# Slot lists ahead of the sort, two whole units in front, and gates after the copies in a two-layer hybrid transformer block with a mixture of experts

## The reference

```python
N_EXPERTS = 64; TOP_K = 6; D_EXPERT = 384; ROUTED_SCALE = 2.5
def swiglu(x, w_gu, w_down):
    g, u = jnp.split(x @ w_gu, 2, axis=-1)
    return (jax.nn.silu(g) * u) @ w_down
# moe_ffn(h, router_w, router_bias, w_gu, w_down, shared_gu, shared_down):
# "Sigmoid top-k routing with selection bias, normalised gates, SwiGLU experts, plus a shared expert."
```

## Time and profile before

| | us |
|---|---|
| median of 3 runs | 2852.13 (2843.32 to 2856.85) |
| time of the profiled execution | 2859.29 |
| span of its trace | 2857.5 |
| TensorE busy in it | 2446.7 |
| VectorE busy in it | 739.8 |
| ScalarE busy in it | 443.8 |
| GpSimd busy in it | 323.4 |

### The profile page before, as it was taken

The page is one execution under the profiler, slowest core; times in us unless marked ns, Lnnn a source line. Parts: engine busy times, 40 slices in busy tenths (PEclk is TensorE's granted clock), DMA queues, the critical chain, the costliest instruction groups (busy, mean ns, idle before and its releaser), DMA issues. The chain is left out here.

```text
span 2857.5 us, 36782 instructions
## 1 busy us (share of the span) xinstructions
PE 2446.7 (86%) x15205; PEld 1334.6 (47%) x15205; DVE 739.8 (26%) x1589; ACT 443.8 (16%) x901; POOL 323.4 (11%) x380
## 2 busy tenths in 40 slices
PE   4999978898989998988985798999897888888885
PEld 2457834554544444444432355875543434443332
DVE  1373523336111111111110445454410111111111
ACT  1233232310000000000000132343000000000000
POOL 0006200000011111110100002400011110010000
PEclk8999987898999999999997899999899999999998
DMA  8000077434699999999995600013599999999993
GB/s 296 30 15 32 3 274 244 164 121 154 246 426 423 412 398 416 400 402 396 394 409 214 222 30 30 4 64 112 226 415 427 421 421 421 415 410 413 411 415 135
DMA packets 126587, 775.99 MB, mean 272 GB/s; under 512 B 36760, under 2 KB 45096, under 8 KB 69968
## 3 DMA queue, kind: packets, MB, share of 16 engines
q1 hardware_dynamic: 103376, 735.75, 63.9%
q0 software_dynamic: 23040, 37.82, 3.5%
HBM read 770.98 MB, written 44.44 MB: 285 GB/s over the span
## 5 line engine op out<-in xcount | busy, mean ns | idle before, releaser
L1419 PE MATMUL banks<-arena,htreg 128*64 128x384 f32 (+1 forms) x4288 | 928.3, 524 | 182.8 <-DMA arena<-in_exp_w_gu 169.6
L1419 PEld LDWEIGHTS banks<-arena,htreg 128*64 128x64 f32 (+1 forms) x4288 | 455.9, 157 | 624.4 <-issue 403.9
L1440 PE MATMUL banks<-arena,modreg 128*64 128x512 f32 (+1 forms) x1608 | 436.2, 602 | 20.7 <-issue 16.7
L2150 DVE TENSOR_TENSOR modreg<-modreg,banks 128x384 f32<-128x384 f32 x80 | 44.3, 554 | 1058.3 <-ACT modreg L1712 1058.2
L1440 PEld LDWEIGHTS banks<-arena,modreg 128*64 128x64 f32 (+1 forms) x1608 | 153.4, 149 | 246.2 <-issue 241.6
L2439 POOL DMA_INDIRECT htreg<-h_d,lsg x74 | 76.3, 1031 | 1064.3 <-PE banks L1400 920.4
L989 PE MATMUL banks<-arena,htreg 128*128 128x512 f32 (+3 forms) x480 | 159.7, 492 | 0.0
L2285 DVE COPY modreg<-banks 128x512 f32<-128x512 f32 x74 | 51.2, 692 | 317.6 <-PE banks L1440 317.6
L1712 ACT ACTIVATE modreg<-banks 128x384 f32<-128x384 f32 x80 | 39.2, 491 | 602.3 <-PE banks L1419 602.3
L2445 POOL DMA_INDIRECT y_d<-modreg,lst x74 | 73.4, 992 | 475.1 <-DVE modreg L2285 474.5
L989 PEld LDWEIGHTS banks<-arena,htreg 128*128 128x128 f32 x480 | 90.0, 191 | 65.5 <-issue 61.5
(11 more groups left out here) (393 smaller groups left out, 2228.3 us busy)
## 6 DMA issues: line engine op xcount, KB each, us to landing
arena<-in_exp_w_gu SPq DMA_DIRECT2D x256, 1536.0 KB, 23.6
arena<-in_exp_w_down SPq DMA_DIRECT2D x128, 1536.0 KB, 23.6
modreg<-in_w_mod SPq DMA_DIRECT2D x40, 1024.0 KB, 5.0
arena<-y_d SPq DMA_DIRECT2D x6, 3072.0 KB, 12.7
modreg<-mod_d SPq DMA_DIRECT2D x20, 512.0 KB, 6.2
arena<-in_w_in SPq DMA_DIRECT2D x4, 2048.0 KB, 9.2
arena<-in_w_out SPq DMA_DIRECT2D x2, 4096.0 KB, 14.7
arena<-in_w_mod SPq DMA_DIRECT2D x6, 1024.0 KB, 9.3
```

The lines of the kernel that those rows point to most:

```text
L1419: last = mm(gu_bank(n, half)[rows, 0:DE], src[:, k, rows], up4[q][:, i, DE * half:DE * (half + 1)], start=(k == 0), stop=(k == KD - 1))
L1440: last = mm(ps[4 + half][rows, :], actT[:, k, rows], dn3[q][:, k, 512 * half:512 * half + 512], start=(k == 0), stop=(k == KE - 1))
```

## The change

It reorders work at the start of each layer's experts; no arithmetic is added or removed.

- `work(l)` puts two whole units in front in both layers. Layer 0 has that already; layer 1 becomes `S S w w p p p p p p p p p p p p p p w ...`. The first two routed units then need ranks 0 and 1 only, which the sort's first round gives.
- VectorE does the sort's first round right after the counts, signals it, makes the slot lists, and does rounds 2 to 8 after them. SyncE waits for the second signal before the loads of r2.
- In layer 1 TensorE makes the slot lists between S0's down projection and S1's projections, and r0's transposes come between S1's projections and S1's `act_transposed` and down projection.
- On VectorE r0's transposes are copied before the gates are made; in layer 1 also before S1's output is copied.

```diff
@@ work(l)
         EARLY = 2
+        FIRST = 2
...
-            order = [whole.pop(0) for _ in range(NOUT[l] - EARLY)]
+            order = [whole.pop(0) for _ in range(FIRST)]
@@ SyncE, the loop over CHUNKS
                     if n not in experts:
+                        if n == ROUTED_AT[l][FIRST]:
+                            sp.wait_ge(sorted_ready.sem, sorted_ready.at(l, 2))
@@ TensorE
-                unit_up(0, between=positions if n_t == 2 else None)
-                if n_t > 2:
+                if n_t == 2:
+                    unit_up(0, between=positions)
+                    ranks()
+                    act_transposed(0)
+                    unit_down(0)
+                    lists_by_expert()
+                    lists_by_unit()
+                    unit_up(1)
+                    unit_transposed(EARLY)
+                    act_transposed(1)
+                    unit_down(1)
+                else:
+                    unit_up(0)
                     positions()
-                act_transposed(0)
-                unit_down(0)
-                ranks()
-                unit_up(1, between=lists_by_expert if n_t == 2 else None)
-                if n_t > 2:
+                    act_transposed(0)
+                    unit_down(0)
+                    ranks()
+                    unit_up(1)
                     lists_by_expert()
-                lists_by_unit()
-                act_transposed(1)
-                unit_down(1)
-                unit_transposed(EARLY)
+                    lists_by_unit()
+                    act_transposed(1)
+                    unit_down(1)
+                    unit_transposed(EARLY)
@@ VectorE
+                def sorted_round(j):
+                    link(dve.max(out=next8, in_=left_of[0]))
+                    ins = dve.max_index(out=eid[:, 8 * j:8 * j + 8], in_max=next8, in_values=left_of[0])
+                    if j in (0, NE // 8 - 1):
+                        ins.then_inc(sorted_ready.sem, 1)
+                        dve.wait_ge(sorted_ready.sem, sorted_ready.at(l, 1 if j == 0 else 2))
...
+                sorted_round(0)
...
-                src = key
-                for j in range(NE // 8):
...
-                    if j == 3 and n_t == 2:
-                        unit_times(0)
-                shared_out(0)
+                if n_t == 2:
+                    unit_times(0)
+                else:
+                    shared_out(0)
                 dve.wait_ge(rank_psum.sem, rank_psum.at(l, 1))
...
                 ts(lsg1[:, 0:U_], lst1[:, 0:U_], 3, None, ALU.logical_shift_right).then_inc(lists_ready.sem, 1)
-                unit_times(1)
-                shared_out(1)
-
-                for i in range(n_t):
-                    link(tt(ohp, onehot[:, i], bc(scores[:, i, :], 1, TOPK), ALU.mult))
...
+                if n_t == 2:
+                    shared_out(0)
+                else:
+                    unit_times(1)
+                for j in range(1, NE // 8):
+                    sorted_round(j)
+                if n_t == 2:
+                    unit_times(1)
+
+                def gates_made():
+                    for i in range(n_t):
...
-                unit_copied(EARLY)
+                if n_t == 2:
+                    unit_copied(EARLY)
+                    shared_out(1)
+                else:
+                    shared_out(1)
+                    unit_copied(EARLY)
+                gates_made()
                 overflow_addresses()
```

More of the change, by code:

```diff
@@ L617, in build @@
         chunk_loaded = [sig(f"chunk_loaded{q}", [len(in_slot(l, q)) for l in LAYERS], 16) for q in range(SLOTS)]
-        sorted_ready = sig("sorted_ready", one)
+        sorted_ready = sig("sorted_ready", [2] * DEPTH)
         lo_used = sig("lo_used", NW)
@@ L2183, in _ @@
                 ts(beats[lo64], key[lo64], keycol[lo64], None, ALU.is_lt).then_inc(beats_ready.sem, 1)
+                left_of = [key]
+                def sorted_round(j):
[5 more added lines that the diff above has]
+                    else:
+                        link(ins)
+                    if j < NE // 8 - 1:
+                        link(dve.match_replace(out=left, in_to_replace=next8, in_values=left_of[0], imm_value=-1e9))
+                        left_of[0] = left
+                sorted_round(0)
                 link(ts(row64[lo64], key[lo64], keycol[lo64], None, ALU.is_gt))
@@ L2226, in _ @@
                 ts(lsg1[:, 0:U_], lst1[:, 0:U_], 3, None, ALU.logical_shift_right).then_inc(lists_ready.sem, 1)
-                unit_times(1)
-                shared_out(1)
-                for i in range(n_t):
-                    link(tt(ohp, onehot[:, i], bc(scores[:, i, :], 1, TOPK), ALU.mult))
-                    link(red(gate[:, i, 0:TOPK], ohp, AX, ALU.add))
-                link(red(gatesum[:, nt_], gate[:, nt_, 0:TOPK], AX, ALU.add))
-                link(dve.reciprocal(gatesum[:, nt_], gatesum[:, nt_]))
-                link(stt(gate[:, nt_, 0:TOPK], gate[:, nt_, 0:TOPK], ROUTED, bc(gatesum[:, nt_], 2, TOPK),
-                         ALU.mult, ALU.mult))
+                if n_t == 2:
[8 more added lines that the diff above has]
+                    for i in range(n_t):
+                        link(tt(ohp, onehot[:, i], bc(scores[:, i, :], 1, TOPK), ALU.mult))
+                        link(red(gate[:, i, 0:TOPK], ohp, AX, ALU.add))
+                    link(red(gatesum[:, nt_], gate[:, nt_, 0:TOPK], AX, ALU.add))
+                    link(dve.reciprocal(gatesum[:, nt_], gatesum[:, nt_]))
+                    link(stt(gate[:, nt_, 0:TOPK], gate[:, nt_, 0:TOPK], ROUTED, bc(gatesum[:, nt_], 2, TOPK),
+                             ALU.mult, ALU.mult))
                 def overflow_addresses():
```

## The result

The changed kernel took 2860.98 us in the median (2854.53 to 2869.22) where the one before took 2852.13; the ratio is 1.0033, 95% interval 1.0021 to 1.0046. A second measurement gave 1.0018 (1.0004 to 1.0031). So it is slower by 5 to 9 us, less than the 0.5% that I called a difference, and on the side that was forecast (+5.3 us, 2857.4).

The account below looks back on a forecast made before the run. The stream of expert weights over DMA was taken to bound layer 1; layer 0's -4.6 us and layer 1's +9.9 us sum to +5.3 us on the median of 2852.1, giving 2857.4 us, range 2845 to 2868.

Parts of the forecast that it names:

- The bound and the ring behind U: Layer 1: weights set the pace; eight buffer slots free too slowly behind two whole units, so the stream runs 9.9 us later.
- U: Layer 1: start of the first routed unit's projections on TensorE, forecast at 2061.2 instead of 2059.03.
- c14: Layer 1: the fourteenth load of expert weights, which opens the full rate; forecast to flow from U + 37.4, 2098.6.
- The first load: Layer 1: the first expert load goes at about 2018.1 instead of 2026.35, 8.2 us earlier.
- The gather: Layer 1: the first routed unit's gather lands behind the weight loads at 2050.2, bounds 2046.4 and 2052.9.
- c6 and c7: Layer 1: sixth and seventh loads of expert weights, forecast to drain by 2049.9, with the gather landing behind them.
- Layer 0: Start of layer 0's experts: 4.2 us from VectorE's new order plus 0.4 from earlier slot lists, 4.6 us gained.
- The step that had VectorE free at 708.4: Layer 0: after copies, gates and overflow addresses VectorE is free at 708.4, so shared S2 starts at 710.3, not 714.54.
- The early start: Rival, layer 1: the ring never runs dry and 8.2 us of earlier weights stand; total -12.8 us, 2839; chance 0.07.
- The slow clock: Rival, layer 1: TensorE stays at 1.2 GHz through the first two routed units; total +17 us, 2869; chance 0.12.
- The gather did not come early: Rival, layer 1: gather lands early, U near 2058, layer 1 +6.8, sum +2 us, 2854; chance 0.22.
- its gain gone: Rival, layer 0: VectorE's longer queue takes all of the gain; total +9.9 us, 2862; chance 0.06.

Follow-up runs that it names:

- Kernel 2: The kernel before with one edit: two whole units lead in layer 1; ratio 1.0034.
- kernels 1: The changed kernel, but in layer 1 the first routed unit's transposes stand behind S1's down projection again and S1's output is copied first; ratio 1.0006 to before.
- kernel 6: The changed kernel, but in layer 1 SyncE holds the sixth and seventh loads until the first two routed units' gathers have landed; ratio 0.9998 to before.
- kernel 4: The changed kernel, but in layer 1 all eight sort rounds stand ahead of the slot lists and SyncE waits for the last; ratio 1.0050 to before.
- kernel 5: The kernel before with gates behind the copies and overflow addresses behind the first routed unit's product, in both layers; ratio 0.9978.
- kernel 7: The changed kernel's layer 0 with layer 1 of the kernel before (the sort's first round placed ahead of five small operations); ratio 0.9985 to before.
- 8: Kernel 7 with gates behind the copies in layer 1 too and the overflow addresses late in both layers; ratio 0.9963 to before, 2840.92 us.
- kernels 3: The kernel before with one edit: the first routed unit's transposes are copied before the gates are made, in both layers; ratio 0.9981.
- 9: Kernel 8 with, in layer 1, the sixth load held until the first routed unit's gather has landed; ratio 0.9951 to before, 2837.95 us.

## Why the prediction was right, point by point

**The bound and the ring behind U: right.** I said that c14 would flow from U + 37.4, that is at 2098.6 on the clock of the kernel before, 9.9 us late after a credit. The whole units' share of that is the difference in the table's last column but one, 6.4 us (748.6 against 742.3 on average) where my rows gave 7.7. Kernel 2 shows it alone. The early loads are worth nothing beyond what they do to U: 0.6 us at most for 8.1 us, by kernels 1 and 2.

**The first load:** 8.2 us earlier was forecast, 8.7 measured.

**The gather: right, by the rows rather than by the page of the Trainium skill.** I took 2050.2, on the clock of before, for its landing; it landed at 2051.4 (2036.8 + 14.6, the shift between the two traces at S0). With c6 and c7 held it takes 4.4 us from its issue (kernel 6). With two loads issued just ahead it takes 8.3, and 6.4 in kernel 4, where the first of the two had gone 5.9 us before it and not 2.7. Behind the full backlog it takes 9.5 to 9.7 (kernels 5, 7 and 8, where TensorE waited for it and so shows the landing). So the loads in flight set it. The round robin between rings of the Trainium skill ("DMA: Bandwidth & Descriptors", Queues, rings and completion order), as I read it, would have had it land near 2047: no trace here agrees. Even with no weights in flight it took 4.4 us. So my lower bound of 2.7 us was too low, too. It was of a gather that moved no rows: in the 20 us around one of the two, from 640 to 660 us of the kernel before, the queue of the gathers moved 0.00 MB.

**U: right in sum.** 2061.2 forecast, 2061.7 found, with errors of about 1 us each way in the terms, which is luck. I had r0's transposes at 1.16 us and S1's down projection at 8.46; they took 1.97 and 7.25. What I wrote of the 8.46, that it follows from the small gaps before it, was too simple: the same instructions took 8.46 us in kernels 3 and 9 and 5.39 in kernels 5, 7 and 8. Where they are fast TensorE waits for the gather instead, and r0's projections are slow behind that wait (12.84 to 13.08 us in kernels 5, 7 and 8; 10.54 in kernels 3 and 9). That hid in the kernel before, where both ended together, 47.5 us after S0's start.

**Layer 0: right in size, for partly wrong reasons.** I forecast -4.6 us. The trace keeps 3.4 us by r1, kernel 7 measured 4.3 (0 to 8.6 by its interval), and the average of the layer's length over the six kernels with just this layer 0 is 917.6 against 921.1 of the two with the old one, though single traces differ by 6 us. So a gain of some 4 us is likely and not shown clear of the noise. The step that had VectorE free at 708.4, "a little after TensorE has done r0's projections", was off: it fits r0 at the slow clock, 12.49 us. With the gap ahead of it down to 1.38 us r0 ran at 10.59, TensorE was done sooner and then stood for 4.03 us for VectorE, and S2's first half ran slow for it, 8.30 us. S2 still started 6.3 us sooner, where I had 4.6, and lost 2.9 of it to the slow half. The gates and overflow addresses in VectorE's queue cost that; with the addresses moved away, in kernel 5, the half took 5.43 us.

**The sum:** -3.4 and +8.7 give +5.3 by the marks, the forecast's +5.3, but that match is luck: the forecast was -4.6 and +9.9, and the two misses of 1.2 us cancel. It also takes layer 0 at r1's start; at the end of that layer the same two traces differ by only 0.5 us (920.33 and 919.81), which would give +8.2. The two ratios say +9.4 and +5.1. What of the first is more than the marks show is not explained.

**Rivals.** The early start did not carry. The slow clock did not last through r0 and r1: it was 1.00 from 2046 to 2082. The gather did not come early. In none of the traces with the changed layer 0 is its gain gone at r1's start.

## What to carry to other kernels

Where transfers bind a stage and a ring of buffers feeds it, an earlier first transfer is worth only what the ring can hold; past that the time hangs on when the consumer frees its first buffers and how many it frees per microsecond. Work that is light on bytes for its compute does not belong at the front of such a stage, even if its inputs are known first. A small transfer that something waits for should be issued ahead of the bulk loads, not behind them: in kernel 6, holding back 3 MB of weights until the gathers had landed, this layer ended 2.4 us sooner.

## What the runs showed that I had not expected

TensorE's clock at one and the same place, the same instructions with the same waits of 1.41 and 0.67 us ahead of them, was at its lower level for a part of some executions and at the full one throughout in others. S1's down projection in layer 1 took 8.46 us in three traces (before, 3, 9; its granted clock was 0.63 on average, with stretches of 2 us at 0.50, that is 1.2 GHz), 5.39 in three (5, 7, 8; 1.00, that is 2.4 GHz) and 6.80 in one (2; 0.79). Before and in kernel 7 TensorE has the same instructions in the same order in layer 1, so they do not decide it; what does stays open. And r0's gather in layer 1 took from 4.4 to 9.7 us to land, by the loads that were in flight.
